# Scores ahead of a projection's last unit, and no weight unit split on GpSimd: a decoder trunk on one core

## What is computed

```python
def reference(x, norm_g, ffn_w_in, ...):
    for l in range(DEPTH):
        if l == N_A_LAYERS:
            k_sh, v_sh, c_sh = shared_kv(x, kv_norm_g, fox_w_kvf, fox_b_f)
        x = x + 0.5 * swiglu(rms_norm(x, norm_g[l, 0]), ffn_w_in[l, 0], ffn_w_out[l, 0])
        h = rms_norm(x, norm_g[l, 1])
        if l < N_A_LAYERS:
            x = x + nsa_mixer(h, nsa_w_in[l], nsa_cmp_pos[l], nsa_cmp_w1[l], nsa_cmp_w2[l], rel_bias, nsa_w_out[l])
        else:
            x = x + fox_mixer(h, fox_w_q[j], k_sh, v_sh, c_sh, fox_w_out[j])
        x = x + 0.5 * swiglu(rms_norm(x, norm_g[l, 2]), ffn_w_in[l, 1], ffn_w_out[l, 1])
    return rms_norm(x, final_g)

# one head of a mixer, for 128 queries
s = q @ k.T * scale + bias          # "scores"
p = softmax(s)                      # "maxima", "exponentials"
o = p @ v                           # "values"
```

## Time and profile before

| | us |
|---|---|
| median of 3 executions | 1088.95 |
| lowest and highest | 1086.84 and 1091.93 |
| the profiled execution | 1091.58 |
| its span, first to last instruction | 1089.8 |

### The profile page before, as it was taken

One profiled execution on the slowest core, in us unless ns is written; L12 is line 12 of the kernel. 1 busy time (PEld: TensorE's weight loads), 2 busy tenths in 40 slices (PEclk: granted clock), 3 DMA queues, 4 the chain that ended last, 5 costly groups with the idle time before them and its releaser, 6 DMA issues.

```text
span 1089.8 us, 14059 instructions
## 1 busy us (share of the span) xinstructions
PE 1060.1 (97%) x5067; PEld 872.4 (80%) x5067; DVE 612.5 (56%) x844; ACT 522.7 (48%) x751; POOL 89.4 (8%) x112
## 2 busy tenths in 40 slices
PE   8799999999899999999999999999998999999997
PEld 6688888888677888888888878888886788888886
DVE  4444545677767464445556775454557656444454
ACT  7334344666446364443356454444355646444434
POOL 6300000000202100000000192000002000000000
PEclk9899999999889999999999999999999999999999
DMA  9765465456500245555554655555545135555541
GB/s 269 216 208 187 159 231 193 155 176 210 193 1 1 64 163 194 187 191 170 196 185 155 231 194 192 175 191 186 181 155 194 38 97 193 192 182 189 190 171 39
DMA packets 128675, 182.40 MB, mean 167 GB/s; under 512 B 5929, under 2 KB 100241, under 8 KB 128513
## 3 DMA queue, kind: packets, MB, share of 16 engines
q1 hardware_dynamic: 127008, 176.18, 49.0%
q0 software_dynamic: 1456, 5.72, 2.0%
q10 hardware_dynamic: 176, 0.05, 0.0%
HBM read 180.34 MB, written 1.59 MB: 167 GB/s over the span
## 4 chain that ended last, share of the span: by engine, by line
PE 91%; DVE 4%; ACT 2%; DMA 2%; issue 1%; SPq 0%; DVEq 0%; ACTq 0%
PE inb L396 16%; PE inb L398 16%; PE inb L397 16%; PE acc L396 11%; PE acc L398 11%; PE acc L397 11%; DMA raw<-in_ffn_w_in 2%; PE tb L487 2%; PE inb L603 2%; PE tb L588 1%; PE acc L574 1%; ACT work L979 1%; DVE nmx L1360 1%; PE inb L600 1%; DVE work L1357 1%; DVE wlo L1214 1%
## 5 line engine op out<-in xcount | busy, mean ns | idle before, releaser
L1220 DVE TENSOR_TENSOR wlo<-raw,whi 128x2048 fp32r<-128x2048 f32 x108 | 248.6, 2302 | 247.4 <-ACT whi L864 247.4
L864 ACT CAST whi<-raw 128x2048 fp32r<-128x2048 f32 x108 | 206.5, 1912 | 238.6 <-PE acc L398 117.1
L396 PE MATMUL inb<-whi,thi 128*128 128x512 f32 x784 | 308.1, 393 | 2.0 <-DVE wlo L1214 2.0
L398 PE MATMUL inb<-whi,tlo 128*128 128x512 f32 x784 | 306.1, 390 | 0.0
L397 PE MATMUL inb<-wlo,thi 128*128 128x512 f32 x784 | 306.0, 390 | 0.0
L396 PEld LDWEIGHTS inb<-whi,thi 128*128 128x128 f32 x784 | 147.9, 189 | 32.8 <-issue 2.6
L398 PEld LDWEIGHTS inb<-whi,tlo 128*128 128x128 f32 x784 | 147.7, 188 | 31.3
L397 PEld LDWEIGHTS inb<-wlo,thi 128*128 128x128 f32 x784 | 147.9, 189 | 30.5
L1214 DVE TENSOR_TENSOR wlo<-raw,whi 128x2048 fp32r<-128x2048 f32 x55 | 129.1, 2353 | 46.9 <-ACT whi L858 46.6
L396 PE MATMUL acc<-whi,ghi 128*128 128x512 f32 x320 | 129.0, 403 | 0.0
L398 PE MATMUL acc<-whi,glo 128*128 128x512 f32 x320 | 125.6, 392 | 0.0
(11 more groups left out here) (235 smaller groups left out, 1008.3 us busy)
## 6 DMA issues: line engine op xcount, KB each, us to landing
raw<-in_ffn_w_in SPq DMA_DIRECT2D x176, 512.0 KB, 4.7
raw<-in_ffn_w_out SPq DMA_DIRECT2D x88, 512.0 KB, 4.0
raw<-in_nsa_w_in SPq DMA_DIRECT2D x20, 512.0 KB, 4.2
raw<-in_fox_w_kvf SPq DMA_DIRECT2D x16, 512.0 KB, 4.5
raw<-in_nsa_cmp_w SPq DMA_DIRECT2D x8, 512.0 KB, 4.4
raw<-in_nsa_w_out SPq DMA_DIRECT2D x8, 512.0 KB, 4.4
raw<-in_fox_w_q SPq DMA_DIRECT2D x8, 512.0 KB, 4.4
raw<-in_fox_w_out SPq DMA_DIRECT2D x8, 512.0 KB, 4.5
```

Source lines behind the costliest of these rows:

```text
L396: pe.matmul(o, lh, rh, start=start, stop=False, skip_group_check=True)
L398: return pe.matmul(o, ll, rh, start=False, stop=stop, skip_group_check=True)
L864: act.copy(whi[u % RING][:, :], raw[u % RING][:, :]).then_inc(s_hi, 1)
L1220: dve.tensor_tensor(wlo[u % RING][:, :], raw[u % RING][:, :], whi[u % RING][:, :].bitcast(F32), ALU.subtract).then_inc(s_lo, 1)
```

## The change

In both mixers the last unit of the query projection and the first scores change places on TensorE. In NSA, `scores(0)` come ahead of the unit, `turn_probs(0)` right behind it, then the compressed layer, `scores(1)`, `values(0)`, the last two rounds and `cmp_scores`, which was inside the loop at i = 1 and now runs by pairs of heads, with the wait for the last rounds' copies in its middle. In FOX, `scores(16)` and `scores(17)` come ahead of the unit, with a wait for the copies of round 16 in front; turn and values of item 16 behind it. ScalarE and VectorE follow this order: maxima and exponentials of the first item (FOX: of the first two) are ahead of the query chunk's copy. In FOX they are also ahead of the cast and the subtraction of unit `U_FOXQ + 5`. The loops start at i = 1.

`split` is gone from GpSimd. The two units are cast by `hi` on ScalarE and subtracted by `lo` on VectorE, in `between` at i = 12 in NSA and at i = 4 in FOX.

```diff
-                for i in range(count + 1):
+                for i in range(1, count + 1):
...
-                    if i >= 1:
+                    if i >= 2:
                         values(n0 + i - 1, n0, v(i - 1))
...
             unit(U_NSAQ[1], 0, 0, acc[2:4])
             turn_hidden(1)
-            unit(U_NSAQ[1], 0, 1, acc[2:4])
-            pe.wait_ge(s_ra, 10)
-            pe.wait_ge(s_rd, 10)
...
-                for t in range(NT):
-                    for p in range(H // 2):
+                for p in range(H // 2):
+                    if p == H // 4:
+                        rounds_copied(12)
+                    for t in range(NT):
...
-            scores(0, 0, 0)
+            rounds_copied(10)
+            scores(0, nsa_keys(0), 0)
+            unit(U_NSAQ[1], 0, 1, acc[2:4])
+            turn_probs(0, 0)
             pe.wait_ge(s_hidc, 2)
             cmp_layer2()
             copied(5)
+            scores(1, nsa_keys(1), 1)
+            values(0, 0, nsa_values(0))
             pair_round(10, xn, 2)
             pair_round(11, xn, 3)
...
-                  {0: lambda: rounds_copied(12), 15: lambda: project_first(U_NSA_OUT, 0)},
-                  {1: cmp_scores, 4: cmp_turn, 6: lambda: cmp_values(0), 7: lambda: cmp_values(1),
+            cmp_scores()
+            items(0, nsa_keys, nsa_values, 16,
+                  {15: lambda: project_first(U_NSA_OUT, 0)},
+                  {4: cmp_turn, 6: lambda: cmp_values(0), 7: lambda: cmp_values(1),
...
             pair_round(16, xn, 0)
             pair_round(17, xn, 1)
+            rounds_copied(17)
+            scores(16, 0, 0)
+            scores(17, 1, 1)
             unit(U_FOXQ, 1, 1, inb)
-            pe.wait_ge(s_ra, 17)
-            pe.wait_ge(s_rd, 17)
-            scores(16, 0, 0)
+            rounds_copied(18)
+            turn_probs(16, 16)
             copied(11)
+            values(16, 16, fox_values(0))
             pair_round(18, xn, 2)
             pair_round(19, xn, 3)
...
             cmp_hidden_copy(1)
+            act.activation(junk[:, 0:1], epst[:, :], ACT.Exp)
             hi(U_NSA + 15)
-
-            act.activation(junk[:, 0:1], epst[:, :], ACT.Exp)
+            exps(0)
             chunk_q(acc[2], 1, U_NSA + 14)
+            pt_copy(0)
+            exps(1)
             q_half(10, 2)
             q_half(11, 3)
...
+            items(0, 16, {2: cmp_exp, 5: cmp_copy, 11: lambda: o_hi(0, 0), 12: lambda: hi(U_NSA_OUT + 2), 13: lambda: o_hi(1, 0),
...
             q_half(16, 0)
             q_half(17, 1)
+            act.activation(junk[:, 1:2], epst[:, :], ACT.Exp)
+            exps(16)
+            exps(17)
             hi(U_FOXQ + 5)
-            act.activation(junk[:, 1:2], epst[:, :], ACT.Exp)
             chunk_q(inb[0], 1, U_FOXQ + 4)
+            pt_copy(16)
...
             add_max(0, 0, lambda h: bias[:, h, P:2 * P])
+            lo(U_NSA + 15)
+            chunk_q(acc[3], 1, U_NSA + 14)
+            pt_copy(0)
+            add_max(1, 1, lambda h: bias[:, h, P:2 * P])
+            cmp_keys_values()
+            output(0, 0, 1, True)
             q_half(10, 2)
             q_half(11, 3)
-            cmp_keys_values()
...
+                   8: lambda: cmp_gated(2), 9: lambda: cmp_gated(3), 11: lambda: o_lo(0, 0), 12: lambda: lo(U_NSA_OUT + 2),
...
+            dve.wait_ge(s_decay, H // 4)
+            add_max(16, 0, lambda h: decay0[:, h, :])
+            add_max(17, 1, lambda h: decay0[:, h, :])
             lo(U_FOXQ + 5)
             chunk_q(inb[1], 1, U_FOXQ + 4)
-            dve.wait_ge(s_decay, H // 4)
-            add_max(16, 0, lambda h: decay0[:, h, :])
+            pt_copy(16)
+            output(16, 0, None, True)
...
+                  {3: lambda: o_lo(0, 4), 4: lambda: lo(U_FOX_OUT + 2), 5: lambda: o_lo(1, 4), 7: lambda: o_lo(2, 4)})
...
-                pool.tensor_copy(whi[u % RING][:, :], raw[u % RING][:, :]).then_inc(s_hi, 1)
...
-                pool.tensor_tensor(wlo[u % RING][:, :], raw[u % RING][:, :],
-                                   whi[u % RING][:, :].bitcast(F32), ALU.subtract).then_inc(s_lo, 1)
...
-            split(U_NSA_OUT + 2)
...
-            split(U_FOX_OUT + 2)
```

More of the change, by code:

```diff
@@ L733, in _, with rounds_copied, nsa_keys, nsa_values @@
             turn_hidden(1)
-            unit(U_NSAQ[1], 0, 1, acc[2:4])
-            pe.wait_ge(s_ra, 10)
-            pe.wait_ge(s_rd, 10)
+            def rounds_copied(n):
+                pe.wait_ge(s_ra, n)
+                pe.wait_ge(s_rd, n)
+            def nsa_keys(i):
+                return i // 2
+            def nsa_values(i):
+                g = i % 8 // 2
+                return lambda k, h: vd[:, k, i // 8, g * DH:(g + 1) * DH]
+            def fox_values(i):
+                return lambda k, h: vf[:, k, (2 * i + h) * DH:(2 * i + h + 1) * DH]
             def cmp_layer2():
@@ L835, in _ @@
             pair_round(17, xn, 1)
+            rounds_copied(17)
+            scores(16, 0, 0)
+            scores(17, 1, 1)
             unit(U_FOXQ, 1, 1, inb)
-            pe.wait_ge(s_ra, 17)
-            pe.wait_ge(s_rd, 17)
-            scores(16, 0, 0)
+            rounds_copied(18)
+            turn_probs(16, 16)
             copied(11)
+            values(16, 16, fox_values(0))
             pair_round(18, xn, 2)
             pair_round(19, xn, 3)
-            items(16, lambda i: i, lambda i: (lambda k, h: vf[:, k, (2 * i + h) * DH:(2 * i + h + 1) * DH]), 8,
-                  {0: lambda: rounds_copied(20), 7: lambda: project_first(U_FOX_OUT, 4)},
+            items(16, lambda i: i, fox_values, 8,
+                  {1: lambda: rounds_copied(20), 7: lambda: project_first(U_FOX_OUT, 4)},
                   {3: lambda: turn_o(0, 4), 5: lambda: turn_o(1, 4), 7: lambda: turn_o(2, 4)})
@@ L987, in items @@
             def items(n0, count, between):
-                exps(n0)
-                for i in range(count):
+                for i in range(1, count):
                     pt_copy(n0 + i)
@@ L1118, in cmp_copy @@
                 act.copy(pcT.rearrange("p c n -> p (c n)"), inb[1][0:HN, :]).then_inc(s_cpc, 1)
-            items(0, 16, {2: cmp_exp, 5: cmp_copy, 11: lambda: o_hi(0, 0), 13: lambda: o_hi(1, 0),
+            items(0, 16, {2: cmp_exp, 5: cmp_copy, 11: lambda: o_hi(0, 0), 12: lambda: hi(U_NSA_OUT + 2), 13: lambda: o_hi(1, 0),
                           15: lambda: o_hi(2, 0)})
             o_hi(3, 0)
-            act.wait_ge(s_hi, U_NSA_OUT + 3)
             hi(U_NSA_OUT + 3)
@@ L1167, in _ @@
             q_half(17, 1)
+            act.activation(junk[:, 1:2], epst[:, :], ACT.Exp)
+            exps(16)
+            exps(17)
             hi(U_FOXQ + 5)
-            act.activation(junk[:, 1:2], epst[:, :], ACT.Exp)
             chunk_q(inb[0], 1, U_FOXQ + 4)
+            pt_copy(16)
             q_half(18, 2)
             q_half(19, 3)
-            items(16, 8, {3: lambda: o_hi(0, 4), 5: lambda: o_hi(1, 4),
+            items(16, 8, {3: lambda: o_hi(0, 4), 4: lambda: hi(U_FOX_OUT + 2), 5: lambda: o_hi(1, 4),
                           7: lambda: o_hi(2, 4)})
             o_hi(3, 4)
-            act.wait_ge(s_hi, U_FOX_OUT + 3)
             hi(U_FOX_OUT + 3)
@@ L1485, in _ @@
             lo(U_NSA + 14)
-            lo(U_NSA + 15)
-            chunk_q(acc[3], 1, U_NSA + 14)
             def cmp_keys_values():
@@ L1622, in _ @@
             items(16, 8, lambda i: i, lambda h: decay0[:, h, :], lambda i: None,
-                  {3: lambda: o_lo(0, 4), 5: lambda: o_lo(1, 4), 7: lambda: o_lo(2, 4)})
+                  {3: lambda: o_lo(0, 4), 4: lambda: lo(U_FOX_OUT + 2), 5: lambda: o_lo(1, 4), 7: lambda: o_lo(2, 4)})
             o_lo(3, 4)
-            dve.wait_ge(s_lo, U_FOX_OUT + 3)
             lo(U_FOX_OUT + 3)
@@ L1711, in _ @@
                              bias[:, :, P + end:P + end + 6 * CMP_STRIDE + 1:CMP_STRIDE]).then_inc(s_biasc, 1)
-            def split(u):
-                pool.wait_ge(s_raw[u % RING], 32 * (u // RING + 1))
-                pool.wait_ge(s_used, u - RING + 1)
-                pool.wait_ge(s_hi, u)
-                pool.tensor_copy(whi[u % RING][:, :], raw[u % RING][:, :]).then_inc(s_hi, 1)
-                pool.wait_ge(s_lo, u)
-                pool.wait_ge(s_hi, u + 1)
-                pool.tensor_tensor(wlo[u % RING][:, :], raw[u % RING][:, :],
-                                   whi[u % RING][:, :].bitcast(F32), ALU.subtract).then_inc(s_lo, 1)
-            split(U_NSA_OUT + 2)
             for c, (t, e) in enumerate(CMP_PIECES):
```

7 lines of the change are left out of this document (removed).

## The result

The changed kernel takes 1100.08 us (median of 5 executions, 1095.78 to 1102.09) and the kernel before, on the same chip, 1091.68 us (1086.84 to 1091.93). The ratio is 1.0086, with a 95% interval of 1.0062 to 1.0111: slower by more than the forecast of 1093.8, and past the upper end of its range, 1098.5. The profiled execution of the changed kernel took 1095.78 us, its span is 1094.0; it is the fastest of the five.

The account below looks back on a forecast made before the run. TensorE, busy 97% of the span, bounds the kernel; only its stops and half clock can be won. 1091.6 - 7.8 - 1.9 + 3.75 + 3.75 = 1089.4, plus 4.4 for two clock falls: 1093.8 us, range 1086 to 1098.5.

Parts of the forecast that it names:

- What held the small negation: NSA front: GpSimd's subtraction for an output unit held VectorE's negated maximum, 4.46 us instead of 0.17.
- The NSA front, -7.8: NSA, up to scores(5): scores(0) ahead of the unit remove the 4.07 us stop, scores(5) at 306.0, 7.8 us earlier.
- rival B: Clock falls everywhere, also in the FOX front (1.7) and at the compressed scores (2.4): 1097.9 us, slower; chance 0.22.
- The FOX front, -1.9: FOX, up to turn_probs(18): a new 3.1 us stop at values(16), yet turn_probs(18) 1.9 us earlier.
- The ends, +3.75 each: Both loops: late cast and subtraction delay turn_probs(14) and (22) by 3.75 us each; clock falls add 2.2 at each.
- The rule for the clock: TensorE's clock: by the skill page alone, busy compressed scores cost nothing; the rows disagreed, so 2.4 us stayed in the bound.
- Rival A: TensorE's clock stays up through the shorter stops: 1089.4 us; chance 0.15.
- C: Loop ends: the late splits hide and cost TensorE nothing: 1081.9 us, or 1084 with a fall, faster; chance 0.12.
- D: Fronts: the gains don't come because the change doesn't remove the wait: 1099.1 us, slower; chance 0.07.

Follow-up runs that it names:

- e1: Kernel before with old fronts, only the two splits moved from GpSimd to ScalarE and VectorE in steps 12 and 4: 1095.53 us, ratio 1.0039.
- e4: Changed kernel with unread matmuls filling TensorE's three new stops, ahead of scores(15), scores(23) and values(16): 1091.37 us, ratio 1.0009 to the kernel before.
- e6: Changed kernel with the cast and subtraction of the two output units moved behind the last item: 1086.04 us, ratio 0.9967 to the kernel before.
- e7: As e6, but with the FOX front in the old order and only the NSA front new: 1083.34 us, ratio 0.9949 to the kernel before.
- e8: Changed kernel built and run a second time, unedited: 1097.59 us, ratio 1.0095 to the kernel before.

## Why the prediction was wrong

- **What held the small negation** was right: with GpSimd's split gone, all 24 take 0.17 us (e1 too, with the old order).
- **The NSA front, -7.8, is the step that failed.** It measured -4.67. The step let the compressed scores run at full clock ("3.5 at full") and the loop begin at 295.7. They took 5.26 us, most of it at half clock, scores(2) came at 297.03, and scores(2) and the turn behind them ran at half clock too. That is the second half of rival B, which the forecast kept for the bound at 2.4 us. The miss is 3.1 us, more than that. Where the half clock lasted 3.4 us instead of 6.8 (e4, e6, e7), the front took 28.5 us, 1.6 less; whether full clock would bring the other 1.5, down to the predicted 27.0, no run shows, since in all thirteen traces the clock falls within the compressed scores. The condition was in the rows: the same compressed scores had run at half clock before, with TensorE busy. The waits were right in kind and smaller in size: 0.56 for 0.8, 0.56 and 0.44 for 1.3 and 0.6.
- **The FOX front, -1.9,** measured -0.47. The new stop was there, 2.74 for 3.1, and so was the wait of 0.64 for the copies at scores(16) (predicted 0.8) and the wait at turn_probs(18), 1.01 for 1.3. What the sum lacks is the fall behind values(16), again rival B, priced at 1.7: e6, with the same stop of 2.74 and no fall, takes 20.03 us for the piece, 2.1 less than before, and the changed kernel's 21.67 is 1.64 more.
- **The ends, +3.75 each,** measured 3.42 each, and the falls behind them 1.6 each instead of 2.2: 5.23 and 5.30 for 5.95. The order of work ahead of the stop was the one drawn. e6 against e8 gives 5.24 us for the FOX end, and 3.54 for the NSA end with a fall of 1.7 in e6's loop against it.
- **Rival B** was the true case in the trace: the clock fell at all four places. The forecast's sum is +2.2 in the mixers; with 1.7 and 2.4 for the two more falls it is +6.3, against +5.4 measured. Of four places where the clock could fall, the forecast let it fall at two. The measured 1100.08 us lies above even rival B's 1097.9.
- **The rule for the clock.** The Trainium skill (TensorE: Matmul & The Clock Gate, What's actually happening) has idleness throttle the array and activity release it. e4 agrees where three stops are concerned: without idleness no fall. It does not tell the fall in the compressed scores, which in the changed kernel came behind a wait of 0.56 us and in the kernel before behind none, nor the one in the loops of e4, e6 and e7, behind a wait of 1.5 us that brought none in the other traces.
- **Rival A** (the clock stays up) is refuted by the windows, C (the late splits hide) by the two stops of 3.42 us and e6 against e8, D by the negations.

What the traces don't reach: the profiled executions differ by 4.2 us and the medians by 8.4 (the interval allows 6.8 to 12.1). The four executions without a profile have a mean clock of 0.982 to 0.987, the profiled one 0.988. At equal clock, 0.987 or 0.988, the kernel before took 1091.8 us (median of 24 executions) and the changed one 1096.8 (of 4, e8's with them): 5.0 us. So 5 us are explained place by place, and the other 3 go with a lower mean clock in executions that have no trace. Where those falls lie stays open. That e4's median clock is 0.993 suggests that they belong to the stops, but doesn't show it.

## What to carry to other kernels

When work moves off a slow engine, its new place matters more than the freed engine: look for a spot behind the last item that TensorE waits for, not for idle time between two items, because a queue in order turns 4.2 us of work into a 3.4 us stop. Price a stop on TensorE with the half clock behind it, at full if dense matmuls follow and at little if the next turns hang on another engine anyway. And where sparse matmuls ran at half clock before the change, count on it after the change: here they did in all thirteen traces. Compare the pieces of a trace and not only its sums, since a fall in a place that nobody edited is worth 1.6 us either way.
